# A hybrid backbone step on one core: the backward decay sums move from GpSimd to ScalarE and PSUM, and the row transfers follow the sums

## What is computed

```python
acum = jnp.moveaxis(jnp.cumsum(dtc * A.reshape(G, HG), axis=2), 2, -1)
seg = jnp.where(causal, acum[..., :, None] - acum[..., None, :], -jnp.inf)
cb = jnp.einsum('bcign,bcjgn->bcgij', Cc, Bc)
w_intra = cb[:, :, :, None] * jnp.exp(seg)
y_diag = jnp.einsum('bcghij,bcjghp->bcighp', w_intra, dtx)
...
y_f, s_f = ssd_chunked(x, dt_f, A[0], B, C, init_f)
y_b, s_b = ssd_chunked(x[:, ::-1], dt_b[:, ::-1], A[1], B[:, ::-1], C[:, ::-1], init_b)
y = y_f + y_b[:, ::-1] + p['d_skip'].astype(jnp.float32)[:, None] * x.astype(jnp.float32)
```

## Time and profile before

| | us |
|---|---|
| median of 3 runs | 1441.94 |
| lowest, highest | 1439.14, 1447.15 |
| the profiled execution | 1442.76 |
| its span, first to last instruction | 1441.0 |
| its mean granted TensorE clock | 0.995 of full |

### The profile page before, as it was taken

The page is one execution under the profiler, slowest core; times in us unless marked ns, Lnnn a source line. Parts: engine busy times, 40 slices in busy tenths (PEclk is TensorE's granted clock), DMA queues, the critical chain, the costliest instruction groups (busy, mean ns, idle before and its releaser), DMA issues.

```text
span 1441.0 us, 20909 instructions
## 1 busy us (share of the span) xinstructions
PE 1411.1 (98%) x8209; PEld 1307.1 (91%) x8209; DVE 915.1 (64%) x1515; ACT 672.8 (47%) x1252; POOL 112.3 (8%) x102
## 2 busy tenths in 40 slices
PE   7999999999999999999999999989999999999998
PEld 3988888888899998999989998889889999999998
DVE  6677565765566676767666875666746675556562
ACT  4746545343635425252536565453436453434352
POOL 0001102220001000000010111041300010000000
PEclk9999999999999999999999999999999999999999
DMA  9665427665346667755335432345443433444441
GB/s 364 186 218 172 127 74 238 200 204 161 103 132 228 209 233 246 242 165 155 118 99 180 118 109 74 90 159 157 151 118 116 125 125 120 129 121 128 123 127 44
DMA packets 191192, 222.97 MB, mean 155 GB/s; under 512 B 11262, under 2 KB 156790, under 8 KB 191094
## 3 DMA queue, kind: packets, MB, share of 16 engines
q1 hardware_dynamic: 191094, 221.64, 48.7%
HBM read 217.58 MB, written 4.03 MB: 154 GB/s over the span
## 4 chain that ended last, share of the span: by engine, by line
PE 87%; issue 4%; DMA 3%; DVE 3%; POOL 1%; SPq 1%; ACT 1%; ACTq 0%; DVEq 0%; POOLq 0%
PE bank L778 23%; PE bank L779 23%; PE bank L780 23%; PE bank L798 2%; PE bank L799 2%; PE bank L800 2%; DMA back_rows<-acs_rows 2%; PE seg_ps L986 1%; PE bank L822 1%; PE y_ps L1012 1%; PE y_ps L1002 1%; PE y_ps L1075 1%; DMA dts<-in_w_mod_dram 1%; POOL back_rows L2316 1%; PE seg_ps L822 1%
## 5 line engine op out<-in xcount | busy, mean ns | idle before, releaser
L1690 DVE TENSOR_TENSOR wlo<-raw,whi 128x1024 fp32r<-128x1024 f32 (+1 forms) x288 | 350.9, 1226 | 208.7 <-ACT whi L1242 206.9
L778 PE MATMUL bank<-ahi,whi 128*128 128x384 f32 (+1 forms) x1280 | 444.5, 347 | 0.9 <-DVE wlo L1690 0.9
L1242 ACT CAST whi<-raw 128x1024 fp32r<-128x1024 f32 (+1 forms) x288 | 296.2, 1035 | 306.3 <-PE bank L780 209.3
L779 PE MATMUL bank<-alo,whi 128*128 128x384 f32 (+1 forms) x1280 | 433.3, 339 | 0.0
L780 PE MATMUL bank<-ahi,wlo 128*128 128x384 f32 (+1 forms) x1280 | 433.3, 339 | 0.0
L778 PE MATMUL bank<-bhi,whi 128*128 128x384 f32 x768 | 264.9, 345 | 0.0
L779 PE MATMUL bank<-blo,whi 128*128 128x384 f32 x768 | 259.7, 338 | 0.0
L780 PE MATMUL bank<-bhi,wlo 128*128 128x384 f32 x768 | 259.5, 338 | 0.0
L778 PEld LDWEIGHTS bank<-ahi,whi 128*128 128x128 f32 x1280 | 241.9, 189 | 11.6 <-issue 8.9
L779 PEld LDWEIGHTS bank<-alo,whi 128*128 128x128 f32 x1280 | 242.0, 189 | 3.7 <-issue 3.1
L780 PEld LDWEIGHTS bank<-ahi,wlo 128*128 128x128 f32 x1280 | 241.6, 189 | 0.0
(11 more groups left out here) (280 smaller groups left out, 1431.5 us busy)
## 6 DMA issues: line engine op xcount, KB each, us to landing
raw<-in_w_mlp_dram SPq DMA_DIRECT2D x128, 512.0 KB, 3.6
raw<-in_w_in_dram SPq DMA_DIRECT2D x104, 512.0 KB, 4.0
raw<-in_w_mod_dram SPq DMA_DIRECT2D x64, 512.0 KB, 6.0
raw<-in_w_ssd_o_dram SPq DMA_DIRECT2D x16, 512.0 KB, 3.4
raw<-in_w_out_dram SPq DMA_DIRECT2D x16, 512.0 KB, 3.5
arena_g<-in_w_mod_dram SPq DMA_DIRECT2D x13, 512.0 KB, 4.6
arena_s<-in_w_mod_dram SPq DMA_DIRECT2D x12, 512.0 KB, 6.8
ahead_rows<-acs_rows SPq DMA_DIRECT2D x12, 512.0 KB, 5.1
```

Source lines behind the costliest of these rows:

```text
L778: nc.tensor.matmul(dst, uh[:, k, tm_cols(m)], hi[k0 + k], start=first and k == 0, stop=False)
L779: nc.tensor.matmul(dst, uh[:, k, tm_cols(m)], lo[k0 + k], start=False, stop=False)
L1242: nc.scalar.copy(dst, src).then_inc(hi_ready, 1)
L1690: nc.vector.tensor_tensor(rest, full, top.bitcast(F32), ALU.subtract).then_inc(lo_ready, 1)
```

## The change

GpSimd's `back_rows_sum` is removed. ScalarE's `row_sum` takes a direction e: for e = 1 it reads `back_rows` and writes `seg_ps`, in eight instructions, after the pick before has read `seg_ps`. `row_sums` runs e = 1, then e = 0. `pick` reads `seg_ps`. `load_rows` waits for the backward sums (`back_sum`) in place of `picked`. The transfers are called after fills 11, 13, 15, 17, 19 and 23 in place of 11, 14, 15, 18, 23 and 25. On ScalarE the sums of a tile move forward, and so does the first exponential of each group; the sums of the first tile of group 1 move into the end of group 0. On VectorE the pick of tile 2 goes ahead of `y_diag` of tile 1. TensorE's instructions stay.

```diff
-ROWS_AFTER = (11, 14, 15, 18, 23, 25)
+ROWS_AFTER = (11, 13, 15, 17, 19, 23)
...
-                for e, used in enumerate((ahead_sum, picked)):
+                for e, used in enumerate((ahead_sum, back_sum)):
...
-                def row_sum(g, t):
+                def row_sum(g, t, e):
 
                     n = g * TT + t
-                    act.wait_ge(to_loaded[0], (l * 6 + n + 1) * 16)
-                    if n >= 2:
+                    act.wait_ge(to_loaded[e], (l * 6 + n + 1) * 16)
+                    if e and n:
+                        act.wait_ge(picked, l * 6 + n)
+                    if n >= 2 and e == 0:
                         act.wait_ge(ydiag_done, l * 6 + n - 1)
                     for h in range(HG):
-                        a = head_at(t, 0, g) + h
-                        ins = nc.scalar.activation(ew[:, n % 2, h, :], to_rows[0][:, tm_cols(h)], ACT.Identity, bias=lead[:, a:a + 1])
-                    ins.then_inc(ahead_sum, 1)
+                        dst = seg_ps[:, h // 4, tm_cols(h % 4)] if e else ew[:, n % 2, h, :]
+                        a = head_at(t, e, g) + h
+                        ins = nc.scalar.activation(dst, to_rows[e][:, tm_cols(h)], ACT.Identity, bias=lead[:, a:a + 1])
+                    ins.then_inc((ahead_sum, back_sum)[e], 1)
+
+                def row_sums(g, t):
+
+                    row_sum(g, t, 1)
+                    row_sum(g, t, 0)
...
+                row_sums(0, 0)
                 for g in range(2):
...
                     fill(slot[0])
-                    row_sum(g, 0)
                     keep(1, st[:, 0, :], st_ready, (l * 2 + g) * 2 + 1)
+                    decay_exp(g, 0)
                     fill(slot[1])
                     keep(2, st[:, 1, :], st_ready, (l * 2 + g) * 2 + 2)
-                    decay_exp(g, 0)
+                    row_sums(g, 1)
                     fill(slot[2])
-                    row_sum(g, 1)
                     fill(slot[3])
                     decay_exp(g, 1)
+                    row_sums(g, 2)
                     fill(slot[4])
-                    row_sum(g, 2)
                     keep(5, stage[:, 1, :], state_staged, (l * 2 + g) * 2 + 1)
                     keep(6, stage[:, 2, :], state_staged, (l * 2 + g) * 2 + 2)
                     decay_exp(g, 2)
-                    fill(slot[5] + slot[8] + slot[6] + slot[7])
+                    fill(slot[5] + slot[8])
+                    if g == 0:
+                        row_sums(1, 0)
+                    fill(slot[6] + slot[7])
...
                     nc.vector.copy_predicated(ew[:, (g + t) % 2], backward.unsqueeze(1).to_broadcast([P, HG, P]),
-                                              to_rows[1].rearrange("p (h i) -> p h i", i=P)).then_inc(picked, 1)
+                                              seg_ps[:].rearrange("p b (h i) -> p (b h) i", i=P)).then_inc(picked, 1)
...
                     fill(slot[4])
+                    pick(g, 2)
                     y_diag(g, 1)
-                    pick(g, 2)
                     fill(slot[5])
...
-                    back_rows_sum(g, 0)
                     to_end(0, 2, 1, None if g == 0 else -11 + 6)
                     to_end(1, 1, 0, None if g == 0 else -11 + 7)
-                    back_rows_sum(g, 1)
```

More of the change, by code:

```diff
@@ L2309, in skip_rows @@
                     weighted(dtx[:, n % 2, :], skips[:, g, t, :], g, t).then_inc(xd_ready, 1)
[L2311 to L2317, removed]
                 for g in range(2):
@@ L2334, in _ @@
                     to_end(1, 0, 1, 5)
-                    back_rows_sum(g, 2)
                     skip_rows(g, 2)
```

## The result

| | before | after |
|---|---|---|
| median, us | 1444.07 | 1446.7 |
| lowest, highest | 1439.14, 1447.15 | 1444.58, 1449.11 |
| runs | 20 | 20 |
| profiled execution (its span) | 1442.76 (1441.0) | 1444.58 (1442.8) |

The account below looks back on a forecast made before the run. TensorE, with matmuls in 98% of the span, bounds the kernel. Old losses of 18.1 us against new ones of 17.8 (layer 0 5.5, layer 1 12.3) net -0.3, giving 1442 us, range 1433 to 1450.

Parts of the forecast that it names:

- Old waits for `next_state`: TensorE's seven idle times in both scans, 11.5 us, six naming `next_state`; claimed to go, but for about 0.9 us.
- Old clock loss: Both scans: half-speed matmuls after three old waits, 6.6 us lost; claimed to go, with 1.6 us lost at two new waits.
- New waits: TensorE's added idle time in both scans, from ScalarE's and SyncE's new orders: 14.6 us without clock loss.
- Place A: Start of each scan: sums ahead of first weight cast; waits 3.6 us plus 1.6 for clock (layer 1), 1.9 (layer 0).
- Place B: Layer 1, end of group 0: sums with late rows hold up fill 23's cast; wait 4.2 us plus 1.6 for clock.
- Place C: Layer 0, SyncE's queue: rows ahead of state stores, loads and fill 24's weight; wait 2.4 us, then 1.2 more.
- Rival 1: Waits at Place B and Place C stay small through early rows and quicker stores: 1433.6 us, chance 0.19.
- Layer 1's exponential: Layer 1, group 1: the decay exponential, now ahead of a cast, makes the weighing 0.4 us late.
- Eight back sums: ScalarE's eight back sums into PSUM take 2.44 us, like the ahead sums; bounds 2.2 to 3.1 us.
- Rival 3: Slower by the clock: longer or additional slow stretches behind new waits in both scans, 1450 us, chance 0.13.

Follow-up runs that it names:

- Experiment 5: Kernel before, with only the back sums moved to ScalarE into `seg_ps` and back rows waiting for them; row transfers keep their places: ratio 1.0017.
- Experiment 6: Kernel before, with only the rows of tile 1 called one unit earlier in both groups, GpSimd still summing: ratio 0.9988 (0.997 to 1.0006).
- experiment 9: Kernel before, GpSimd kept, with tile 1 rows and group 1's tile 2 rows earlier and one `next_state` ahead of the weighing: ratio 0.9942.
- experiment 8: The changed kernel profiled once more, unedited: span 1444.2 us.
- experiment 3: Changed kernel, with the row transfers of group 1, tile 1 called after fill 20 in place of 19: ratio to the kernel before 1.0008.
- Experiment 2: Changed kernel, with ScalarE's sums of group 1, tile 0 moved behind the cast for fill 23: ratio to the kernel before 0.998.
- experiment 7: Changed kernel with its three costly orders mended, plus two VectorE reorders (weighing before splits, `next_state` before weighing): median 1427.43 us, ratio to the kernel before 0.989.
- experiment 10: Kernel of experiment 7, with ScalarE's back sums in place in SBUF and rows released by the pick: median 1430.4 us, ratio to the kernel before 0.9911.

## Why the prediction was right, and where it was not

It said 1442, range 1433 to 1450, most likely within 0.5%. The ratio of 1.0026 is 3.7 us more than no change; the forecast was 0.3 less. By its own terms the scan of layer 0 was given 5.5 us for the old 9.6 (6.2 of waits, 3.4 of clock), -4.1, and layer 1 12.3 for 8.5, +3.8; they were -2.65 and +4.42. That layer 0 gained and layer 1 lost more came out as worked out. That the total lies near no change is partly luck: two misses, of the waits and of the clock, stand below.

- **Old waits for `next_state`: right.** They went, but for the 0.30 where 0.9 was said. Which part of the change did it was told too simply. Experiment 5 shows that engine and bank alone lose. Experiment 6 shows that earlier rows alone lose again what they win, partly to GpSimd beside VectorE, partly to ahead sums whose rows are late. With one order more on VectorE (experiment 9) they win half. No run has engine and earlier rows without the new orders on ScalarE, so the share of those is not shown.
- **Old clock loss, 6.6 us, exchanged for 3.2: not borne out.** In the profiled execution it was 2.5 for 6.6. On average there is no such gain. (1 - mean clock) x time is 7.5 us for the 20 runs of the changed kernel, and 6.8, 7.1 and 7.5 for the 29, 23 and 11 runs of the kernel before that were timed beside the experiments. These are upper bounds of the loss, as the clock is low in part of a wait too: in experiment 8 TensorE was idle in 3.9 of the 7 us of the slow stretch at B.
- **New waits, 14.6 us by its own terms: 17.0,** and 16.7 in experiment 8. Most of the miss is B.
- **Place A: waits right, clock wrong.** 3.38 for 3.6, 2.21 for 1.9 (0.3 of it since the back rows landed 0.57 us after ScalarE was ready). The 1.6 us for the clock did not come in the profiled execution and did in experiment 8, so the term holds in one execution and not in the next, and was taken for a certainty.
- **Place B: mechanism right, 4.2 us was too low.** The wait was 5.86. The rows were issued at 978 and took 8.7 us, as the old 8.3 said. The copy, split and `y_off` followed as worked out. What failed is the time at which TensorE arrives. Counted from the start of the scan, the bank came free 1.1 us earlier than forecast, but TensorE stood there 2.8 us earlier: 1.6 of it is A's slow clock, which didn't come, 0.2 A's shorter wait, 0.6 the wait on `next_state`. Of the last 0.4, 0.3 is in the forecast itself: it says that TensorE is there at about 994.0, and its own terms give 994.95 + 2.9 + 1.6 - 1.2 - 1.2 - 3.3 = 993.7. The sum of the two terms, 5.2 + 5.8 = 11.0, was 3.38 + 5.86 + 2.5 = 11.7. The slow clock behind B was 2.5 for 1.6. A loss that is left out at one place is partly paid at the next.
- **Place C: right in size and in cause.** 2.65 for 2.4. The rows waited until 276.9 and not 280.3, but TensorE was 3 us earlier too. Both are the shift that its own terms for layer 0 imply (5.2 won, 1.9 added) and that this place was reckoned without; it cancels in the difference. The tail of 1.2 came as 1.19 + 0.68; experiment 3 shows that the 0.68 is not C's.
- **Rival 1** wanted early rows for a small B. Experiment 2 leaves the rows late, moves the sums past one cast, and has no wait at B at all.
- **Layer 1's exponential, 0.4 late:** 0.77, in every edit of the changed kernel but experiments 7 and 10, which weigh earlier; in experiment 5, with the exponentials in their old order, it is not there.
- **Eight back sums, 2.44 us:** 2.41. ScalarE's cost in itself was nothing, as said; the cost was what stood behind it.
- **Rival 3 (1450, the clock):** experiment 8 meets its condition, three of four new waits brought a slow stretch. Its span is 1444.2, 1.4 over the first execution of the same program, not 8, and 3.2 over the kernel before. The slowest of the 20 runs took 1449.11.

So little if any of the 3.7 us is the clock (7.5 us against 6.8 to 7.5, above). It is waits: 17.0 and 16.7 against 11.5 us, each from a single execution. What stays open is why these 5 us of waits are only 3.7 in the ratio. Slow stretches that lie partly in the longer waits would do it, but no run shows that.

## What to carry over

Before a long or waiting instruction goes ahead of others on an in-order engine, list what is queued behind it and when the next engine needs each. Here two casts moved ahead of sums and one transfer called a unit later were the difference between 0.3% slower and 1% faster. Moving work to another engine lost alone, moving its inputs earlier gave nothing alone that is clear of noise, and a kernel with both, and with the orders that fit, won: such a change is not judged by its parts. And when a forecast adds a term for the clock, take it as an average over executions, not from one profile.

## What was not expected of the hardware

**Whether a wait of 2 to 4 us loses the clock changes from one execution to the next.** Experiment 8 shows it for one program at one place. Over the profiles here, 24 waits of TensorE in the scans were of 2 us or more. The granted clock fell to 0.50 behind 18: all four over 5 us, and 14 of the 20 between 2.1 and 3.7. It stayed at 1.00 behind 2.21, 2.65, 2.67, 3.00, 3.38 and 3.39. It also fell behind 1.78, 1.80 and 1.83, not behind 1.82, and in experiment 9 behind 1.59 and 0.67 and behind 1.00 and 0.67, each pair close together. Most slow stretches cost 1.7 us or up to 3.4. The spread of the runs fits: 14 us wide for the kernel of experiment 6, with five waits of 1.78 to 2.14, and 1.4 us wide for that of experiment 7, with none over 0.74 (12 runs against 4). The mean clock of each run bears it out: in experiment 6 the run of 1434.8 us had 1.000, and the five of 1444.4 to 1448.6 had 0.991 or 0.992, which is some 12 to 13 us of their time; in experiment 7 all had 0.998 or more.

**PSUM as ScalarE's destination shortens one instruction, not a row of them.** Grouped rows of after (busy, mean ns), then one row of eight in place in SBUF of experiment 10:

```profile
L1534 ACT ACTIVATE arena_s<-ahead_rows,dts 128x128 f32<-128x128 f32 x96 | 29.2, 388 | 0.0
L1534 ACT ACTIVATE seg_ps<-back_rows,dts 128x128 f32<-128x128 f32 x96 | 29.0, 355 | 13.4 <-DMA back_rows<-acs_rows 12.7 <-ACT arena_s L1550 0.7
```

```profile
229.30 2.45 ACT L1532 ACTIVATE back_rows<-back_rows,dts 128x128 f32<-128x128 f32 x8
```

33 ns less for one, and 2.41 against 2.45 us for eight. The Trainium skill (ScalarE: Activation LUTs, "Step-by-step: what each stage is for") calls PSUM the destination of lower latency. The trace agrees for the single instruction, 33 ns, and shows that a row hardly gains: 0.04 us for eight back to back.

**GpSimd beside VectorE** made single operations of VectorE 1.6 to 3.3 times as long: a pick 2.07 and 1.30, a weighing 2.80 and 1.23, the first operation of a `next_state` 2.27 and 0.68. The weighing of 2.80 in experiment 6 ended 1.08 us after the GpSimd addition beside it, and the 2.27 of experiment 9 ended 0.54 after its own (1.90 from 253.54 on). Both are a little less than the operation takes alone, as if it had stood until GpSimd was done; no run tests this. VectorE's busy time fell by 10 us when twelve GpSimd additions left.
